# Stick-breaking attention for two heads at once: plain float32 products on halves of the array, a second sigmoid, and the next pair's projections between them

## What is computed

```
def stick_breaking_attention(q, k, v):
    ...
        z = jnp.einsum('bhtd,bshd->bhts', q_blk, k).astype(jnp.float32) * (D ** -0.5)
        causal = kpos[None, :] < qpos[:, None]
        log_keep = jnp.where(causal, -jax.nn.softplus(z), 0.0)
        between = lax.cumsum(log_keep, axis=3, reverse=True) - log_keep
        w = jnp.where(causal, jnp.exp(jax.nn.log_sigmoid(z) + between), 0.0)
        return jnp.einsum('bhts,bshd->bhtd', w.astype(v.dtype), v)
...
    o_b = o_b * jax.nn.silu(gate_b)
    y_b = jnp.einsum('bse,ed->bsd', o_b, w_up_b)
    merged = jax.nn.sigmoid(mg_a) * y_a + jax.nn.sigmoid(mg_b) * y_b
    sub = jnp.einsum('bsd,de->bse', merged, w_out)
    return layer_norm(DEEPNORM_ALPHA * x + sub, ln_g, ln_b)
```

## Time and profile before

| what | value |
|---|---|
| runs | 861.12 us median of 3 (857.84 to 861.34) |
| profiled execution, first to last instruction | 860.0 us |
| TensorE busy, weight loads busy | 802.8 us (93%), 659.7 us (77%) |
| VectorE, GpSimd, ScalarE busy | 465.4, 369.3, 352.0 us |
| mean granted TensorE clock | 0.982 of full |
| DMA | 51.0 MB, mean 59 GB/s |

### The profile page before, as it was taken

How to read it: one execution, slowest core, us unless ns; L and a number is a source line. 1 busy time by engine, 2 the same in 40 slices (tenths; PEclk the granted TensorE clock), 3 DMA queues, 4 the chain that set the end, 5 groups by cost and what they waited for, 6 DMA issues and landing times.

```text
span 860.0 us, 10173 instructions
## 1 busy us (share of the span) xinstructions
PE 802.8 (93%) x3872; PEld 659.7 (77%) x3872; DVE 465.4 (54%) x620; ACT 352.0 (41%) x644; POOL 369.3 (43%) x321
## 2 busy tenths in 40 slices
PE   8999999999879987998899888999999999999996
PEld 6887877787767776777777666888888888888885
DVE  6377555375886588658865887411202202254453
ACT  7587454543545344534453445312111111144220
POOL 0222111235696669666866687322122222210392
PEclk9999999999999999999999999999999999999999
DMA  9141100013001200120022000111111111124251
GB/s 329 39 123 32 42 27 26 29 48 96 1 25 42 82 1 26 52 71 0 25 59 65 0 26 26 50 50 50 49 50 50 50 49 50 50 72 173 75 204 65
DMA packets 16912, 51.01 MB, mean 59 GB/s; under 512 B 2272, under 2 KB 2272, under 8 KB 16864
## 3 DMA queue, kind: packets, MB, share of 16 engines
q1 hardware_dynamic: 16864, 50.37, 17.7%
HBM read 40.92 MB, written 4.19 MB: 52 GB/s over the span
## 4 chain that ended last, share of the span: by engine, by line
PE 65%; POOL 21%; issue 7%; DVE 4%; ACT 2%; DMA 1%; POOLq 0%; SPq 0%; ACTq 0%; DVEq 0%
PE ps L78 20%; PE ps L80 20%; PE ps L79 20%; POOL keep L313 7%; POOL beta L309 5%; POOL o_t L327 3%; POOL sig_m L322 3%; POOL w_lo L289 2%; PE ps L1139 1%; PE ps L1122 1%; PE ps L1207 1%; PE ps L1150 1%; DVE stick_a L880 1%; ACT w_hi L402 1%; DVE beta L889 1%
## 5 line engine op out<-in xcount | busy, mean ns | idle before, releaser
L289 POOL TENSOR_TENSOR w_lo<-raw,w_hi 128x1024 fp32r<-128x1024 f32 (+1 forms) x53 | 120.2, 2268 | 348.5 <-ACT w_hi L402 347.7
L78 PE MATMUL ps<-x_hi,w_hi 128*128 128x512 f32 x672 | 267.6, 398 | 1.5 <-DVE x_lo L797 1.5
L80 PE MATMUL ps<-x_hi,w_lo 128*128 128x512 f32 x672 | 263.5, 392 | 0.0
L79 PE MATMUL ps<-x_lo,w_hi 128*128 128x512 f32 x672 | 263.3, 392 | 0.0
L78 PEld LDWEIGHTS ps<-x_hi,w_hi 128*128 128x128 f32 x672 | 127.9, 190 | 27.9 <-DVE x_lo L797 2.4
L80 PEld LDWEIGHTS ps<-x_hi,w_lo 128*128 128x128 f32 x672 | 127.0, 189 | 27.6
L79 PEld LDWEIGHTS ps<-x_lo,w_hi 128*128 128x128 f32 x672 | 127.5, 190 | 24.6
L975 DVE TENSOR_TENSOR sig_m<-sig_m,ps 128x512 f32<-128x512 f32 x16 | 10.9, 681 | 168.1 <-PE ps L80 168.1
L402 ACT ACTIVATE w_hi<-raw 128x1024 fp32r<-128x1024 f32 x49 | 51.9, 1060 | 113.3 <-PE ps L80 112.9
L1176 PE MATMUL ps<-ident,beta 128*128 128x128 f32 x288 | 49.9, 291 | 37.8 <-DVE w_t L896 30.1
L567 ACT ACTIVATE w_t<-ps 128x512 fp32r<-128x512 f32 (+1 forms) x96 | 46.6, 490 | 89.5 <-PE ps L1176 89.0
(11 more groups left out here) (112 smaller groups left out, 1183.9 us busy)
## 6 DMA issues: line engine op xcount, KB each, us to landing
raw<-in_w SPq DMA_DIRECT2D x56, 512.0 KB, 3.2
o_t<-in_xt SPq DMA_DIRECT2D x16, 256.0 KB, 5.7
ks<-ks SPq DMA_DIRECT2D x16, 256.0 KB, 4.3
raw<-in_xn SPq DMA_DIRECT2D x8, 512.0 KB, 3.5
out<-o_t SPq DMA_DIRECT2D x16, 256.0 KB, 2.0
raw<-in_w SPq DMA_DIRECT2D x4, 256.0 KB, 5.5
ka<-ka SPq DMA_DIRECT2D x4, 256.0 KB, 4.3
o_t<-in_cos SPq DMA_DIRECT2D x1, 512.0 KB, 5.2
```

Of the source, the lines that this page charges most:

```text
L78: pe.matmul(out, w_hi, x_hi, start=first, stop=False)
L79: pe.matmul(out, w_hi, x_lo, start=False, stop=False)
L80: return pe.matmul(out, w_lo, x_hi, start=False, stop=last)
L289: pool.tensor_tensor(w_lo[:, n % 2, cols], raw[:, n % 2, cols], w_hi[:, n % 2, cols].bitcast(F32), ALU.subtract).then_inc(lo_first if part ...
```

## The change

The steps of branch B are redone. A step now takes **both heads of a pair** and the same two query blocks, as a big unit (1024 - 128 j columns) and a small one (128 (j + 1) columns); there are 16 steps, s = 4 p + j, where there were 32 of one head.

- Keys, queries, values and weights are kept once, as plain float32. A head's scores are one product over 64 rows of the array, a head's values one product on 64 columns of it, and the two heads use the two halves. No low parts of them are made, and the keys aren't copied by DMA.
- keep is a second sigmoid, of -z, taken from PSUM by ScalarE (`betas`). GpSimd only cuts the diagonal blocks of keep and beta (`cut_causal`, affine_select). VectorE scans keep in place, one scan for each head, and multiplies beta (`break_sticks`).
- ScalarE alone copies the turned blocks; VectorE multiplies a finished output from PSUM by the gate (`gated_out`).
- Between the parts of a step TensorE makes the eighths of one tile (`fill`): in steps 0 to 11 one of the next pair's k, q, v and gate tiles, in steps 12 to 14 a merge gate's. Tile K_B0 + 2 + s = 14 + s belongs to step s. The merge tile (1, 1) is made behind step 15, ahead of the first up-projection, where it was made behind it.

```
+            def cut_causal(s, small):
+                i = 2 * s + small
+                kp, bt = (keep_small, beta_small) if small else (keep_big, beta_big)
+                pool.wait_ge(keep_set, i + 1)
+                kp_d = kp[:, :, 1:P + 1]
+                pool.affine_select(out=kp_d, in_=kp_d, compare_op=ALU.is_gt, fill=1.0, base=0,
+                                   pattern=[[0, 2], [1, P]], channel_multiplier=-1).then_inc(keep_cut, 1)
+                pool.wait_ge(beta_set, i + 1)
+                bt_d = bt[:, :, 0:P]
+                pool.affine_select(out=bt_d, in_=bt_d, compare_op=ALU.is_gt, fill=0.0, base=0,
+                                   pattern=[[0, 2], [1, P]], channel_multiplier=-1).then_inc(beta_cut, 1)
             pool.wait_ge(lo_done, 2)
+            for n in range(2, K_B0 + 3):
                 low_weights(n)
+            for s in range(STEPS):
+                cut_causal(s, False)
+                if s > 0:
+                    low_weights(K_B0 + 2 + s)
+                cut_causal(s, True)
+            for n in range(K_B0 + 2 + STEPS, W_OUT + 1):
                 low_weights(n)
...
+                act.activation(kp[:, :, 1:w + 1], z_both[:, :, 0:w], ACT.Sigmoid,
+                               scale=-SCALE).then_inc(keep_set, 1)
+                act.activation(bt[:, :, 0:w], z_both[:, :, 0:w], ACT.Sigmoid,
+                               scale=SCALE).then_inc(beta_set, 1)
...
+            for s in range(STEPS):
+                betas(s, False)
+                if s > 0:
+                    turned_blocks(s - 1, True)
+                fill_half(s, 0)
+                betas(s, True)
+                if s % 4 == 3 and s < STEPS - 1:
+                    turned_values(s // 4 + 1)
+                turned_blocks(s, False)
+                fill_half(s, 1)
+                if s < STEPS - 1:
+                    weight_hi(K_B0 + 4 + s)
...
+                dve.wait_ge(keep_cut, i + 1)
+                for h in range(2):
+                    stick = kp[:, h, 0:w + 1]
+                    dve.tensor_tensor_scan(stick, stick, stick, 1.0, ALU.mult,
+                                           ALU.bypass).then_inc(scanned, 1)
+                dve.wait_ge(beta_cut, i + 1)
+                dve.wait_ge(scanned, 2 * (i + 1))
+                dve.tensor_tensor(bt[:, :, 0:w], bt[:, :, 0:w], kp[:, :, 0:w], ALU.mult).then_inc(w_ready, 1)
...
+                    for h in range(2):
+                        r = slice(HD * h, HD * h + HD)
+                        last = pe.matmul(ps[:, 2 + 2 * h + at // HALF, 0:m], qs[r, p % 2, P * tb:P * (tb + 1)],
+                                         ks[r, p % 2, P * tb + at:P * tb + at + m], start=True, stop=True)
...
+                for b_ in range(nb):
+                    for h in range(2):
+                        r = slice(HD * h, HD * h + HD)
+                        last = pe.matmul(bank[r, 0:P], v_n[:, p % 2, tb + b_, r], w_t[:, b_, h, :],
+                                         start=b_ == 0, stop=b_ == nb - 1)
...
+            for s in range(STEPS):
+                scores(s, False)
+                fill(s, (0, 1))
+                if s > 0:
+                    turn(s - 1, True, (0, 1))
+                fill(s, (2, 3))
+                if s > 0:
+                    values(s - 1, True)
+                scores(s, True)
+                fill(s, (4, 5))
+                if s % 4 == 3 and s < STEPS - 1:
+                    turn_values(s // 4 + 1)
+                turn(s, False, (0, 1))
+                fill(s, (6,))
+                turn(s, False, (2, 3))
+                fill(s, (7,))
+                values(s, False)
```

More of the change, by code:

```diff
@@ L284, in low_weights @@
-            def low_weights(n, parts=None):
+            def low_weights(n):
                 pool.wait_ge(hi_done, n + 1)
[L287 to L312, removed]
-                pool.tensor_scalar(keep[:, i % 2, at:at + m], bt, -1.0, 1.0, ALU.mult, ALU.add).then_inc(kept, 1)
@@ L677, in _ @@
[L677 to L691 removed]
+            for k in range(2):
+                branch_hi(k)
@@ new lines, in turn @@
+            def turn(s, small, groups):
+                i = 2 * s + small
+                bt = beta_small if small else beta_big
+                nb = unit(s, small)[1]
+                for g in groups:
+                    if g < unit_banks(s, small):
+                        pe.wait_ge(w_ready, i + 1)
+                        bank = ring_bank(("t", i, g))
+                        for b_ in range(2 * g, min(2 * g + 2, nb)):
+                            for h in range(2):
+                                at = P * (2 * (b_ % 2) + h)
+                                last = pe.transpose(bank[:, at:at + P], bt[:, h, P * b_:P * (b_ + 1)], ident[:])
+                        last.then_inc(turned, 1)
@@ new lines, in values @@
+            def values(s, small):
+                i, p = 2 * s + small, s // 4
+                w_t = w_small if small else w_big
+                tb, nb = unit(s, small)
+                bank = ring_bank(("o", i, 0))
+                pe.wait_ge(turned_out, ring_count(RING_AT["o", i, 0], False))
+                for b_ in range(nb):
+                    for h in range(2):
+                        r = slice(HD * h, HD * h + HD)
+                        last = pe.matmul(bank[r, 0:P], v_n[:, p % 2, tb + b_, r], w_t[:, b_, h, :],
+                                         start=b_ == 0, stop=b_ == nb - 1)
+                last.then_inc(o_done, 1)
@@ new lines, in fill @@
+            def fill(s, eighths):
+                p, j = s // 4, s % 4
+                n = pair_tile(p + 1, "kqvg"[j]) if p < PAIRS - 1 else merge_tile(j // 2, j % 2)
+                if p < PAIRS - 1 or j < 3:
+                    for e in eighths:
+                        eighth(n, e, n if p < PAIRS - 1 else USE_U + j)
+            for q in range(4):
+                chunk(K_B0, q)
+            pe.wait_ge(oa_free, NCHUNK)
+            pe.wait_ge(tp_free, 4 + NCHUNK)
+            turn_values(0)
@@ L1282, in up @@
+            for q in range(2):
+                chunk(merge_tile(1, 1), q, USE_U + 3)
+            turn(STEPS - 1, True, (0, 1))
+            chunk(merge_tile(1, 1), 2, USE_U + 3)
+            values(STEPS - 1, True)
+            chunk(merge_tile(1, 1), 3, USE_U + 3)
             def up(j):
```

674 lines of the change are left out of this document (226 added, 448 removed).

## The result

| kernel | median of the runs, us | lowest to highest |
|---|---|---|
| before, beside it on the same chip | 859.48 | 857.27 to 861.34 |
| after (4 runs) | 970.87 | 969.61 to 971.66 |

The change makes the kernel slower: ratio 1.1294 (95% interval 1.1268 to 1.1319), 111 us more where 100 were forecast. The time lies in the range, 11 us above the forecast.

A forecast was written before the change was run, and what follows sets the result against it. The prediction took branch B to be a TensorE stream with holes. It summed 860.0 - 58 + 131 + 22 + 8 = 963 us, said 960 us, and gave 918 to 992 us as its 8 in 10 range.

The forecast's parts named there:

- holes that go, less dearer products: Branch B without waits would shrink from 329.1 us to the 271 its products need, saving 58 us.
- stops, 14: Steps 1 to 14: TensorE waits after the big scores for sigmoids, cuts, scans and GpSimd's low part; 131 us together.
- half clock behind them: Behind each of 14 stops, 3.4 us at 1.2 GHz loses 1.6 us; 22 us in all.
- small waits: Turning the big unit waits for scans and product: about 1 us in step 0, 7 in step 15; 8 us.
- products, 271 us: TensorE's products in branch B after the change were summed to 271 us, against 267 before: no saving by itself.
- GpSimd's cut of beta at 2 us or more under a scan: Sign expected in the changed kernel's profile: GpSimd's cut of beta lasts 2 us or more beside a VectorE scan.
- Taking turns: In each stop GpSimd can't work beside a VectorE scan; queued together they alternate, making 10.4 us at 1024 columns.
- Rival A: Scans don't hold GpSimd up; stops of 7.4 to 6.2 us, 927 us in all; chance 0.18 with its half form.
- its half form: GpSimd takes the low part in the gap between two scans; 935 us; chance within the 0.18 of Rival A.
- Rival C: Faster than before: short stops in the steps, holes worth more, deciding at 3.6 us a step; 810 us without stop; chance 0.05.
- Rival B: Row halves run one after the other, so scores cost 31 us more over 16 steps; 991 us; chance 0.12.
- Rival D: Plain float32 on array halves much dearer or cheaper than read; at half cost 35 us go, to 928; chance 0.03.

The follow-up runs named there:

- e1: Changed kernel with GpSimd taking the low part of the step's tile ahead of both cuts of the big unit; 821.86 us, ratio 0.9569.
- e3: Changed kernel with 28 to 37 extra TensorE products, their results overwritten, filling each of the 14 stops; 940.49 us, ratio 1.0952.
- e4: Changed kernel with each VectorE scan taking only the first 129 columns, output not the reference's; 932.74 us, ratio 1.0852.
- e2: Changed kernel with GpSimd taking the low part between the cut of keep and the cut of beta; 912.39 us, ratio 1.0622.
- e8: On e1, an eighth of a tile stands between the two heads' big scores, so they can't overlap; 852.29 us, ratio 0.9906.
- e6: On e1, all value blocks of the first head come before those of the second, instead of in turn; 839.33 us, ratio 0.9768.
- e5: On e1, a unit's scores are made for one head and then the other, instead of in turn; 820.10 us, ratio 0.9547.

## Why the prediction was right

The time of branch B, as starts of the up-projection show it, grew from 329.1 + 10.9 to 450.6 us, by 110.6. By the forecast's terms:

| term | forecast, us | measured, us | from |
|---|---|---|---|
| holes that go, less dearer products | -58 | -44.5 | 329.1 - 284.6, e1 |
| stops, 14 | +131 | +115.0 | waits of after |
| half clock behind them | +22 | +30.4 | after - e3 |
| small waits | +8 | +8.8 | the other five waits of after |
| sum | +103 | +109.7 | |

- **The bound.** Branch B was a stream with holes, and the holes could be closed: e1 does it. But 45 us were to be had, not 58. The term that was mis-sized is that of products, 271 us: plain float32 on halves costs what was read, at its low end, but a fp32r product next to plain float32 or behind turned blocks costs 0.1 us more, seven times a step, some 10 us. The sum had no term for these places. Another 4 us or so are the half clock in step 15, which the forecast counted only as a wait.
- **The new wait** is where the prediction put it, 14 times, and e1 shows that nothing else makes the kernel slower than before. It was mis-sized by an eighth: at 1792 columns the forecast had 9.7 us, the trace 8.6. The 1.1 us are four small terms: 0.2 before the first scan (the sigmoid starts 0.06 us behind the scores, not 0.3), 0.3 for a cut between the scans that costs VectorE next to nothing (scans and cut take 4.10 us, where 4.03 and 0.4 were counted), 0.3 in the low part (2.1 us behind the second scan, not 2.4), and 0.3 in the signals. One sign failed: "GpSimd's cut of beta at 2 us or more under a scan". It took 1.17 in the mean. The forecast's own sum has it at 1.3: the cut comes at 4.1 us and the first scan ends at 5.0. Another sign was off too: TensorE's busy time was to stay nearly as before, and it is 832.6 us against 802.8, since products at half clock last longer.
- **Taking turns** is the mechanism, and now shown from both sides: with short scans the stops lose 32.6 us (e4), and with GpSimd first by 0.06 us it is the scans that are late (e2). Rival A is not what the changed kernel does, and neither is its half form, the low part in the gap between two scans: it ends 2.1 us behind the second.
- **The clock** was mis-sized the other way: 30 us, not 22. A stop of 7 to 9 us is followed by 4.1 to 5.5 us at 1.2 GHz, not by the 3.4 taken from a 2 us wait.
- **Rival C** put the point from which the change gains at 3.6 us a step. e2, whose stops are 4.5 us each, is still slower than before, and e1, with none, is faster, 822 against the 810 that the rival gave; the 12 us are the 13.6 by which products were sized too low, less 1.6 of small waits. With the measured terms the point lies at (44.5 - 8.8) / 14 = 2.6 us, clock included. **Rival B** priced a head's scores rightly (one head alone takes what both take together, e8), but the halves overlap. **Rival D** is out: values cost the low end of what was taken.

The mechanism was right. That the number came so near is in part luck, since the mis-sized terms nearly cancel: 16 us too many for the stops, against 13.5 and 8 too few for products and clock. And the sum was 963 us; the step from there to 960 had no term behind it.

## What to carry to other kernels

When work is moved, look for the instruction that the waiting engine needs next, and at what now stands ahead of it in its maker's queue; here one line on GpSimd is worth 149 us (970.87 - 821.86), far more than the 45 us that the change saves in branch B. Price a stop with its clock: add some 2 us to each stop of 8 us on TensorE. And two plain float32 products on the two halves of the array cost as much as one, if they stand next to each other in the program; a long run of one half and then of the other loses the overlap (e6).

## What the runs showed of the hardware

- A short GpSimd instruction beside a VectorE scan waits for the scan's end, and a scan waits for a GpSimd instruction in the same way: neither is slowed down in proportion. In after, the cut (0.41 us alone) ends 0.2 us behind the first scan and the low part (2.34 alone) 2.13 behind the second, so 0.2 us of each lie beside the scan. The cut took 0.41 us alone and 1.17 in the mean beside a scan, the low part 2.34 and 4.04 (e4, after); two scans took 4.10 us and 6.24 with a low part ahead of the first (e2). VectorE's product of two operands takes turns with the low part as well: 2.03 us alone (e2), 3.91 beside it (after).
- Row halves and column halves both overlap in full: 1.70 us for one head's scores and for two (e8, e1); for values, a block of both heads costs 0.44 us with the halves apart and 0.22 with them in turn (e6, e1).
- The order of products within a unit of eight records didn't matter, within one of twelve or more it did (e5, e6).
- An fp32r product of 128 x 512 next to plain float32 takes 0.33 us from start to start, one behind turned blocks 0.31, one ahead of them 0.24, all others 0.23 (e1).
- The half clock begins within a stop, not behind it: over the 8.5 us of one in after the mean grant is 0.64 with no product running, and in the 4.6 us behind it 0.55.
